# An expert's rows over 128: blocks of 32 rows with four products side by side, instead of blocks of 64 with two

## The reference, cut to what matters

```
g_prob = softmax(x @ rg_w + rg_b);  g_val, g_idx = top_k(g_prob, 1)            # 4 groups
sel = (x @ re_w + re_b)[8 experts of that group];  e_val, e_idx = top_k(sel, 2)
weights = softmax(e_val) * g_val;  expert = g_idx * 8 + e_idx                  # 32 experts
out[token] += weights * (silu(x @ w1[expert]) * (x @ w3[expert])) @ w2[expert] # w1, w3: 1024x512, w2: 512x1024
```

```
111 121 131 127 111 144 164 163 140 162 167 124 128 132 130 147
 94 133 142 160 135 110 156 128  99 107  82 131  73 143 110  91
```

## Time and profile before

| | us |
|---|---|
| median of 3 runs | 2556.92 (2556.85 to 2564.13) |
| the profiled execution | 2558.19 |
| its span | 2556.5 |
| mixer and merge, up to the start of `route` | 1607 |
| `route` | 1607 to 1658 |
| experts | 1658 to about 2506 |
| final norm and output | to 2556.5 |

### The profile page before, as it was taken

One profiled execution on the slowest core, in us unless ns is written; L12 is line 12 of the kernel. 1 busy time (PEld: TensorE's weight loads), 2 busy tenths in 40 slices (PEclk: granted clock), 3 DMA queues, 4 the chain that ended last, 5 costly groups with the idle time before them and its releaser, 6 DMA issues. The chain is left out here.

```text
span 2556.5 us, 33679 instructions
## 1 busy us (share of the span) xinstructions
PE 2359.6 (92%) x11388; PEld 1851.6 (72%) x11389; DVE 1379.7 (54%) x1970; ACT 1098.2 (43%) x1380; POOL 675.5 (26%) x515
## 2 busy tenths in 40 slices
PE   6978999799999999999999999489999999999991
PEld 5757777688888888888888887367667766677771
DVE  6898575634444444444543444656555555557565
ACT  4523233233333333333333332257556656567663
POOL 3821101100000000000000000096555657558761
PEclk9989999899999999999999999699999999999996
DMA  7864746443364336433462323379778978789987
GB/s 238 317 231 157 263 158 219 108 136 93 109 208 152 93 101 204 142 117 102 126 218 86 100 83 136 124 260 328 255 256 287 321 262 287 255 314 356 316 277 284
DMA packets 311868, 516.30 MB, mean 202 GB/s; under 512 B 33180, under 2 KB 211616, under 8 KB 295392
## 3 DMA queue, kind: packets, MB, share of 16 engines
q1 hardware_dynamic: 290000, 445.59, 49.9%
q0 software_dynamic: 16464, 56.90, 9.1%
q10 hardware_dynamic: 5312, 12.58, 1.3%
HBM read 430.33 MB, written 84.68 MB: 201 GB/s over the span
## 5 line engine op out<-in xcount | busy, mean ns | idle before, releaser
L1503 PE MATMUL mrgps<-xn_hi,w_hi 128*128 128x512 f32 x1024 | 401.3, 392 | 6.8 <-DVE w_lo L1622 6.8
L1503 PE MATMUL mrgps<-xn_lo,w_hi 128*128 128x512 f32 x1024 | 399.5, 390 | 0.0
L1503 PE MATMUL mrgps<-xn_hi,w_lo 128*128 128x512 f32 x1024 | 399.5, 390 | 0.0
L1967 POOL TENSOR_TENSOR w_lo<-w_raw,w_hi 128x1024 fp32r<-128x1024 f32 x128 | 331.4, 2726 | 0.0
L1434 ACT ACTIVATE gt<-mrgps,mb 128x512 f32<-128x512 f32 x128 | 88.3, 690 | 508.7 <-PE mrgps L1503 502.6
L1766 POOL IOTA io_g<- 128x4 f32 x1 | 0.1, 144 | 1109.2 <-POOLq L1230 1109.2
L1962 DVE TENSOR_TENSOR w_lo<-w_raw,w_hi 128x2048 fp32r<-128x2048 f32 x125 | 284.6, 2336 | 0.1
L1639 DVE SCALAR_TENSOR_TENSOR tmp<-gt,mrgps 128x512 f32<-128x512 f32 x96 | 66.0, 687 | 386.6 <-PE mrgps L1503 386.6
L1952 ACT ACTIVATE w_hi<-w_raw 128x2048 fp32r<-128x2048 f32 x128 | 239.1, 1920 | 10.4 <-DMA w_raw<-in_expert_w_dram 10.3
L1503 PEld LDWEIGHTS mrgps<-xn_hi,w_hi 128*128 128x128 f32 x1024 | 192.9, 188 | 47.7 <-issue 8.1
L1503 PEld LDWEIGHTS mrgps<-xn_hi,w_lo 128*128 128x128 f32 x1024 | 192.8, 188 | 40.4
(11 more groups left out here) (425 smaller groups left out, 4306.7 us busy)
## 6 DMA issues: line engine op xcount, KB each, us to landing
w_raw<-in_expert_w_dram SPq DMA_DIRECT2D x192, 1024.0 KB, 7.1
w_raw<-in_merge_gate_w_dram SPq DMA_DIRECT2D x128, 512.0 KB, 4.0
win_hi<-w_in_parts SPq DMA_DIRECT2D x42, 512.0 KB, 3.5
win_lo<-w_in_parts SPq DMA_DIRECT2D x42, 512.0 KB, 4.5
w_raw<-in_branch_w_dram SPq DMA_DIRECT2D x128, 128.0 KB, 4.1
wout<-in_w_out_dram SPq DMA_DIRECT2D x64, 256.0 KB, 4.3
branch_rows<-in_x_dram SPq DMA_DIRECT2D x16, 512.0 KB, 6.0
residual<-branch_rows SPq DMA_DIRECT2D x16, 512.0 KB, 3.3
```

The costliest lines, as they stand in the source:

```text
L1503: last = pe.matmul(bank[:], w[:, u % 2, kk], x, start=(kk == w_tiles[0] and j == 0), stop=(kk == w_tiles[-1] and j == 2))
L1967: eng.tensor_tensor(self.lo2[:, f], self.raw2[:, f], self.hi2[:, f].bitcast(F32), ALU.subtract).then_inc(self.split2, 1)
```

## The change

`HB` goes from 64 to 32, and the tables from 96 to 156 block numbers. The half block becomes a part block (`part_block`) of up to 32 rows. An expert with 129 to 160 rows has one, with 161 to 192 rows two.

In `part_expand` four products stand side by side, each with 32 columns of the array and 256 columns of weights: the two halves of w1 at PSUM partitions 0 to 63, those of w3 at 64 to 127. So the gate is one chain in place of two: one tanh and one copy on ACT, two instructions on DVE (both halves as 64 partitions), one `turn_part_h`, one `part_h`. `part_contract` has four products of 256 columns side by side in place of two of 512. `turn_x` for the next block now stands between `part_expand` and `turn_part_h`. The results leave by four ACT copies in place of two. The first DVE instruction no longer waits for up_rows, the second does. DVE copies 32 rows of x per block instead of 64.

In `route` V, S and U keep their form with 156 columns; U is one buffer for both choices, so the second U waits until PE has read the first; the work area is shared. The slot weights are copied to one more table (`twice`), by two more DVE instructions.

```diff
-HB = P // 2
+HB = P // 4
-NB = 94
+NB = 154
...
-        V, U = sb("V", [P, TT, 2, P], F32R), sb("U", [P, TT, 2, NBT], F32R)
+        V, U = sb("V", [P, TT, 2, P], F32R), sb("U", [P, TT, NBT], F32R)
...
                 s.link(TTc(S[:, :, k], row(io_b[:], NBT), bc(blkf[:, :, k], NBT), ALU.is_equal))
-                s.link(TTc(U[:, :, k], S[:, :, k], bc(io_tok[:], NBT), ALU.mult))
+                if k:
+                    dve.wait_ge(u_read, 1)
+                s.link(TTc(U[:], S[:, :, k], bc(io_tok[:], NBT), ALU.mult))
                 dve.sem_inc(uv_ready, 1)
...
-            s.link(dve.tensor_copy(scales[:], scale_ps[:, 0:NBT]))
+            s.mark(dve.tensor_copy(scales[:], scale_ps[:, 0:NBT]))
+            s.mark(dve.tensor_copy(twice[0:HB], scale_ps[0:HB, 0:NBT]))
+            s.link(dve.tensor_copy(twice[HB:2 * HB], scale_ps[0:HB, 0:NBT]))
...
-            def half_expand(g, e1):
+            def part_expand(g, e1):
                 pe.wait_ge(x_plain, g * 2 + 2)
-                pe.sem_inc(h_ps, 1)
-                for j in range(2):
-                    for k in range(KD):
-                        cols = slice(k % 4 * DE + j * HC, k % 4 * DE + (j + 1) * HC)
-                        for w in range(2):
-                            if j == 0 and k % 4 == 0:
-                                pe.wait_ge(wt.in13[2 * w + k // 4], e1 * 16)
-                            last = pe.matmul(half_ps[j][w * HB:(w + 1) * HB, 0:HC], xT[:, k], wt.raw13[:, 2 * w + k // 4, cols],
+                pe.sem_inc(h_ps, 2)
+                for k in range(KD):
+                    for w in range(2):
+                        if k % 4 == 0:
+                            pe.wait_ge(wt.in13[2 * w + k // 4], e1 * 16)
+                    for w in range(2):
+                        for j in range(2):
+                            at = (2 * w + j) * HB
+                            last = pe.matmul(part_ps[at:at + HB, 0:HC], xT[:, k], wt.raw13[:, 2 * w + k // 4, k % 4 * DE + j * HC:k % 4 * DE + (j + 1) * HC],
                                              start=(k == 0), stop=(k == KD - 1))
...
+            def part_contract(g, e1):
+                pe.wait_ge(y_free, g * 2 + 3)
+                pe.wait_ge(h_split, g * 2 + 3)
+                for f in range(FE):
+                    if f % 2 == 0:
+                        pe.wait_ge(wt.in2[f // 2], e1 * 16)
+                    for c in range(4):
+                        last = pe.matmul(ybank[0][c * HB:(c + 1) * HB, 0:HC], hT[:, f], wt.raw2[:, f, c * HC:(c + 1) * HC],
+                                         start=(f == 0), stop=(f == FE - 1))
+                        if f == FE - 1 and c >= 2:
+                            last.then_inc(y_ps, 1)
+
+            def part_block(g, e1):
+                part_expand(g, e1)
+                pe.wait_ge(x_split, g * 2 + 2)
+                pe.sem_inc(h_turned, 1)
                 turn_x(g + 1, 0)
                 turn_x(g + 1, 1)
-                for f in range(FE):
-                    if f == 1:
-                        turn_h(g, 1)
-                    half_contract(g, f, e1)
+                turn_part_h(g)
+                part_contract(g, e1)
...
+            def part_tanh(g):
+                act.wait_ge(h_ps, g * 3 + 5)
+                act.activation(th[0:2 * HB, 0:HC], part_ps[0:2 * HB, 0:HC], ACT.Tanh, scale=0.5).then_inc(part_tanh_d, 1)
+                act.activation(up_row[:], part_ps[2 * HB:4 * HB, 0:HC], ACT.Copy).then_inc(up_set, 1)
...
+            def part_gate(g):
+                gated_ps = part_ps[0:2 * HB, HC:2 * HC]
+                dve.wait_ge(part_tanh_d, g + 1)
+                dve.scalar_tensor_tensor(gated_ps, th[0:2 * HB, 0:HC], 1.0, part_ps[0:2 * HB, 0:HC], ALU.add, ALU.mult).then_inc(part_gate_d, 1)
+                dve.wait_ge(up_set, g + 1)
+                dve.wait_ge(part_gate_d, g + 1)
+                dve.sem_inc(gated, 1)
+                dve.scalar_tensor_tensor(hg[0:2 * HB, 0], gated_ps, twice[:, ds(g, 1)], up_row[:], ALU.mult, ALU.mult).then_inc(gated, 1)
```

More of the change, by code:

```diff
@@ L1719, in _, with route @@
                 logit(m, t)
-def route(nc, dram, logits, table, dest, scales, ends, wt):
+def route(nc, dram, logits, table, dest, scales, twice, ends, wt):
     with ExitStack() as ctx:
@@ L1743, in route @@
                                                  sb("io_tok", [P, TT]), sb("later_tile", [P, E, TT]))
-        below, ones, minus = sb("below", [P, P]), sb("ones", [P, P]), sb("minus", [P, P])
+        below, ones = sb("below", [P, P]), sb("ones", [P, P])
         cum = sb("cum", [P, E, TT])
@@ L1811, in _ @@
                 for i in range(TT):
-                    last = pe.matmul(tab_ps[:, 0:NBT], V[:, i, k], U[:, i, k], start=(i + k == 0), stop=(i == TT - 1 and k == 1))
-            last.then_inc(tab_ready, 1)
+                    last = pe.matmul(tab_ps[:, 0:NBT], V[:, i, k], U[:, i], start=(i + k == 0), stop=(i == TT - 1 and k == 1))
+                last.then_inc((u_read, tab_ready)[k], 1)
             for k in range(2):
@@ L1967, in write_low2, with run_experts @@
             eng.tensor_tensor(self.lo2[:, f], self.raw2[:, f], self.hi2[:, f].bitcast(F32), ALU.subtract).then_inc(self.split2, 1)
-def run_experts(nc, io, dram, table, dest, scales, ends, wt, out):
+def run_experts(nc, io, dram, table, dest, scales, twice, ends, wt, out):
     HC = 256
@@ L2104, in _ @@
             wt.write_low2(pool, 0)
-            over_blocks(pool, half_block, one)
+            over_blocks(pool, part_block, one)
             total = pool.value_load(ends[0:1, E:E + 1], min_val=1, max_val=NB - 1)
@@ new lines, in part_expand, with turn_part_h @@
+                last.then_inc(h_ps, 1)
+            def turn_part_h(g):
+                pe.wait_ge(gated, g * 2 + 5)
+                for c in range(2):
+                    last = pe.transpose(hbank[0][:, c * P:(c + 1) * P], hg[:, 0, c * P:(c + 1) * P], ident[:])
+                last.then_inc(h_turned, 1)
+            def part_contract(g, e1):
[9 more added lines that the diff above has]
+                            last.then_inc(y_ps, 1)
@@ L2224, in _ @@
             act.sem_inc(h_high, 1)
-            act.sem_inc(y_set, 2)
+            act.sem_inc(y_set, 4)
             def high_x(g, h):
@@ L2261, in half_block @@
                 act.wait_ge(added, g * 16 + 16)
-                for n in range(2):
-                    act.activation(ysb[0:HB, n], ybank[0][n * HB:(n + 1) * HB], ACT.Copy, scale=0.5).then_inc(y_set, 1)
-                act.wait_ge(y_set, g * 2 + 4)
+                for c in range(4):
+                    act.activation(ysb[0:HB, c // 2, c % 2 * HC:(c % 2 + 1) * HC], ybank[0][c * HB:(c + 1) * HB, 0:HC], ACT.Copy, scale=0.5).then_inc(y_set, 1)
+                act.wait_ge(y_set, g * 4 + 8)
                 act.sem_inc(y_free, 2)
@@ L2292, in _ @@
             high_x(0, 1)
-            over_blocks(act, half_block, one)
+            over_blocks(act, part_block, one)
             for i in range(TT):
@@ L2362, in _ @@
             low_x(0, 1)
-            over_blocks(dve, half_block, one)
+            over_blocks(dve, part_block, one)
             s = Steps(dve, c_step)
@@ L2387, in trunk @@
     with ExitStack() as ctx:
-        scales = ctx.enter_context(nc.sbuf_tensor("slot_weights", [P, NB + 2], F32))
-        dest = ctx.enter_context(nc.sbuf_tensor("slot_rows", [P, NB + 2], I32))
-        table = ctx.enter_context(nc.sbuf_tensor("table", [P, NB + 2], I32))
-        ends = ctx.enter_context(nc.sbuf_tensor("ends", [P, E + 1], I32))
         mix_sems = []
@@ L2401, in trunk @@
             with ExitStack() as weights_ctx:
+                scales = weights_ctx.enter_context(nc.sbuf_tensor("slot_weights", [P, NB + 2], F32))
+                twice = weights_ctx.enter_context(nc.sbuf_tensor("part_weights", [2 * HB, NB + 2], F32))
+                dest = weights_ctx.enter_context(nc.sbuf_tensor("slot_rows", [P, NB + 2], I32))
+                table = weights_ctx.enter_context(nc.sbuf_tensor("table", [P, NB + 2], I32))
+                ends = weights_ctx.enter_context(nc.sbuf_tensor("ends", [P, E + 1], I32))
                 wt = ExpertWeights(weights_ctx, nc, io)
-                route(nc, dram, logits, table, dest, scales, ends, wt)
-                run_experts(nc, io, dram, table, dest, scales, ends, wt, out)
+                route(nc, dram, logits, table, dest, scales, twice, ends, wt)
+                run_experts(nc, io, dram, table, dest, scales, twice, ends, wt, out)
 _INS = ["x", "norm1_g", "w_in", "conv_a_w", "pool_w", "pool_b", "pool_scale", "s5_lambda_re", "s5_lambda_im", "s5_log_step",
```

103 lines of the change are left out of this document (38 added, 65 removed).

## The result

The changed kernel takes 2619.62 us (median of 4 runs, 2614.04 to 2625.48) against 2558.24 (2556.85 to 2564.13) for the kernel before on the same chip: a ratio of 1.0238, 95% interval 1.0222 to 1.0254. It is slower by 61 us. The profiled execution has a span of 2620.0 against 2556.5, so 63.5 us are to be found.

A forecast was written before the change was run, and what follows sets the result against it. PE was taken to set the experts' pace, tied with POOL's gather (0.3 us of slack). Route +8, one part block +4 and two part blocks +70 gave +82 on 2558.2: 2640, or 2639 as median; 2590 to 2665 held 8 in 10.

The forecast's parts named there:

- Part block on PE: PE in the experts' part blocks: 0.446 us a four, expand 3.6, contract 1.8; first part block 9.8 instead of 12.9.
- Rival C: PE in part blocks: four products side by side run two by two, block 13.1 long; 2641 to 2650, chance 0.05.
- The long wait: Four experts with two part blocks: PE waits for the gather behind w2's splits; +17.4 each, +70 (43 to 80).
- One part block: The 13 experts with one part block: -4 from shorter experts, +8 from the clock; net +4 (-5 to +12).
- Route: Stage ahead of the experts: larger tables on DVE, wider PE products, two small copies; +8 (+4 to +13).
- Rival A: Experts' stage: the gather always lands in 3.9 us, so waits are shorter; 2576, chance 0.08.
- Rival B: Experts' stage: PE sets the pace throughout, if POOL can issue the gather before T+5; 2540, chance 0.06.

The follow-up runs named there:

- e2: The changed kernel with the eight fours of part_expand computed twice in every part block: 2603.88 us, ratio 1.018 to the kernel before.
- e3: The changed kernel with SP issuing the next w1 and w3 only when the gather has landed: 2604.2 us, ratio 1.0183 to the kernel before.
- e4: The changed kernel with POOL's gather, in experts with part blocks, behind the first of w2's four lo pieces: 2561.97 us, ratio 1.0012 to the kernel before.
- e7: e4 with two of w2's hi pieces (ACT) moved behind part_h and the fourth w1/w3 lo quarter (DVE) behind the gate: 2531.14 us, ratio 0.9906.
- e5: e4 with nine identity products on PE between turn_x and turn_part_h in every part block (the fill): 2547.63 us, ratio 0.9958 to the kernel before.
- e8: The changed kernel, gather where it was, with the nine identity products of e5: 2634.6 us, ratio 1.0304 to the kernel before.
- e11: e7 with the gather ahead of all four of w2's lo pieces instead of behind the first: 2574.96 us, ratio 1.0071 to the kernel before.
- e12: e11 with DVE writing all four lo quarters of w1 and w3 ahead of the part block's gate: 2540.42 us, ratio 0.9925 to the kernel before.
- e10: e7 with the next expert's block numbers read ahead of the full block's work on ACT, DVE and POOL: 2532.79 us, ratio 0.9899.

## Why the prediction was right

The forecast was 2639 with a range of 2590 to 2665; measured 2619.6. It was slower by the mechanism that was named, and by 19 less: 10 lie in the experts with one part block, 4 in those with two, 2 in `route`, and 2 in the mixer, which the change doesn't touch.

- **Part block on PE: right.** 0.446 a four gave 3.6 for the expand and T+9.8 for the end; measured 3.66 and, where the clock stayed up, 9.7 (11.2 in expert 8, where it fell). Rival C (two by two) is out by the record: 64 records of 256 columns in 3.66, half of the earlier trace rows. By the rule of the Trainium skill that was weighed ("TensorE: Matmul & The Clock Gate", Measured speedup vs the span model) the expand would be 4.5, an estimate; the trace shows no such loss for four of 32 columns in float32.
- **The long wait: right, with two sizes off that cancel in part; that the sum came so near is some luck.** Issue at T+15.7 forecast, T+15.5 measured. From the gather's issue to the start of the turning 7.5 was taken, between 3.9 and 8.7; it was 9.1, 9.0 and 9.5 in three experts and 5.0 in the fourth, 2.6 over the forecast in sum. The upper bound was too low: SP's weights were seen as "just filling" the queue, but even 4 MB issued 0.06 to 1.8 us ahead kept the gather's packets away for 4.1 to 4.4 us and then took most of the engines beside them. That a block at half clock would turn the two issues round, in one expert of four, was not foreseen. The other way, from the turning to the full block 4.0 and 3.0 for the clock were forecast; it took 5.9, 5.2, 6.5 and 5.4, with 4.0 at full clock in e2, so the clock cost 1.2 to 2.5 and the sum is 5.1 under the forecast. With the earlier issue that gives +66 against +70.
- **One part block: wrong sign, by 10 us.** This is the term that was wrong: +4 was forecast and -5.5 came. The forecast put the clock's loss behind waits for the gather in the full block (+8). But the wait for the gate, 2.4 in the part block, came first, which the working had (tanh at T+5.5) and did not price as a wait. The clock fell there, in most cases, and the slower last products only used up the slack ahead of the gather: eight of the 13 full blocks then waited under 1 us for the gather where 2.8 was forecast, five 1.7 to 4.7, and only three turned x at half clock behind it.
- **Route: right in kind, +5.7 for +8.** DVE's share was +4.0 for +4.1. PE's products were over-sized: the 16 take 3.70 with 156 columns (3.65 with 96), the 64 take 10.92 (9.94): +1.0 for +4. The two small copies cost 0.6 for 0.3.
- **Rival A** is out as "always" (62 us of waits), but its 3.9 is near what shows wherever no weights are ahead: 4.3 in e3, 4.4 in e2 and 5.0 in expert 9. **Rival B** named the right lever, POOL's order, with a condition that was too strict (T+5): e4 issues the gather at T+8.5, ahead of the weights, and PE never waits for it. Its 2540 needed the clock as well: 2562 without, 2548 with the fill.

## What to carry to other kernels

An engine that works through its program in order and is busy for 58% of the time, as POOL in this stage, can still set the pace, by what stands in its program ahead of one small instruction. Follow the next block's gather back to its issue before the work of the pacing engine is cut, and again after, since a faster engine also moves the loads that compete with it. Where two engines work on elementwise instructions with SBUF operands (DVE and POOL here), look at each pair of them that an edit newly places side by side.

## What the runs showed that was not expected

- An indirect gather of 0.5 MB took 4.2 to 5.0 us from issue to landing without weights ahead of it, and 9.0 to 9.4 with 4 MB issued 0.06 to 1.8 us before it.
- A stand of PE of 2.4 us is followed by a granted clock of 1.00 in some part blocks and of 0.50 in others (1.7 against 3.6 for the same 32 records); with a stand of 1.3 it stayed up in 9 of 10 (e7). Nine useless products in the stand gained 14 us in e5 and, on the path, lost 15 in e8.
- Doubling the products of every part block made the changed kernel about 15 us faster (e2).
- DVE and POOL hold each other up: a DVE instruction of 2.3 us took up to 12.0 beside four of POOL's in a row (e11) and 2.3 in the same experts when it was moved ahead of them (e12), and a POOL copy of 0.18 took 2.83 beside one of DVE's (e10).

What stays open: neither e5's fill nor e7's reordering was tried with blocks of 64, so whether 32 or 64 is the better size at the best order is not known. What decides whether a stand of 2.4 us costs the clock was not found.
